# Attention pairs of the second block: a gate's Silu later in the order, the row maximum taken negated, and a PSUM bank for the second head's output

## The reference

```python
def forgetting_attention(q, k, v, f_logit, b_f):     # 16 heads of 64
    ...
        logits = jnp.einsum('bhqd,bhkd->bhqk', qi, k).astype(jnp.float32) * scale
        logits = logits + (Fi[..., :, None] - F[..., None, :])
        logits = jnp.where(q_pos[:, None] >= k_pos[None, :], logits, -jnp.inf)
        p = jax.nn.softmax(logits, axis=-1)
        return jnp.einsum('bhqk,bhkd->bqhd', p.astype(v.dtype), v)
...
        z = h @ w_in[l]
        u_a, v_a, g_a, q_b, k_b, v_b, g_b, f_b = jnp.split(z, pts, axis=-1)
        y_b = forgetting_attention(q_b, k_b, v_b, f_b, b_f[l]) * jax.nn.silu(g_b)
        y = jnp.concatenate([y_a, y_b], axis=-1) @ w_out[l]
```

## Time and profile before

| | us |
|---|---|
| median of 3 runs | 2638.51 |
| lowest, highest | 2636.88, 2639.52 |
| the profiled execution's own time | 2635.45 |
| its span | 2633.8 |
| pairs of the second block, about | 1991 to 2424 |

### The profile page before, as it was taken

One profiled execution on the slowest core, in us unless ns is written; L12 is line 12 of the kernel. 1 busy time (PEld: TensorE's weight loads), 2 busy tenths in 40 slices (PEclk: granted clock), 3 DMA queues, 4 the chain that ended last, 5 costly groups with the idle time before them and its releaser, 6 DMA issues.

```text
span 2633.8 us, 32288 instructions
## 1 busy us (share of the span) xinstructions
PE 2498.5 (95%) x11864; PEld 2014.6 (76%) x11864; DVE 1322.4 (50%) x1985; ACT 879.2 (33%) x1333; POOL 373.3 (14%) x363
## 2 busy tenths in 40 slices
PE   5899999999998999999999998799999999998997
PEld 2678888787887778888787886588877777776886
DVE  8655543377545655543367545725245444444433
ACT  4422222344322522222344222422224444444321
POOL 6300000012001500000012001203001112122000
PEclk8999999999998999999999998999999999999998
DMA  3355554211222355554211332133321222222332
GB/s 134 120 180 176 175 175 127 80 62 52 84 99 73 127 180 175 176 175 128 80 65 49 120 96 71 48 112 105 100 91 64 73 72 78 70 76 64 112 97 79
DMA packets 79437, 277.75 MB, mean 105 GB/s; under 512 B 8960, under 2 KB 9216, under 8 KB 78976
## 3 DMA queue, kind: packets, MB, share of 16 engines
q1 hardware_dynamic: 62496, 217.49, 25.5%
q0 software_dynamic: 14560, 55.06, 6.2%
q10 hardware_dynamic: 2304, 4.20, 0.4%
HBM read 270.41 MB, written 6.29 MB: 105 GB/s over the span
## 4 chain that ended last, share of the span: by engine, by line
PE 76%; issue 16%; DVE 5%; ACT 1%; POOL 1%; DMA 0%; ACTq 0%; DVEq 0%; SPq 0%; POOLq 0%
PE bank L275 23%; PE bank L277 23%; PE bank L276 23%; PE bank L1621 1%; DVE x_lo L909 1%; POOL sum L360 1%; PE bank L1586 1%; DVE w_lo L270 1%; PE bank L1582 1%; ACT w_hi L260 0%; DVE stats L1160 0%; PE bank L1584 0%; PE bank L1585 0%; PE bank L1587 0%; PE bank L1583 0%
## 5 line engine op out<-in xcount | busy, mean ns | idle before, releaser
L275 PE MATMUL bank<-x_lo,w_hi 128*128 128x512 f32 (+1 forms) x3088 | 1236.5, 400 | 48.1 <-DVE x_lo L909 21.3
L277 PE MATMUL bank<-x_hi,w_hi 128*128 128x512 f32 (+1 forms) x3088 | 1212.4, 393 | 0.0
L276 PE MATMUL bank<-x_hi,w_lo 128*128 128x512 f32 (+1 forms) x3088 | 1211.7, 392 | 0.0
L270 DVE TENSOR_TENSOR w_lo<-w_raw,w_hi 128x1024 fp32r<-128x1024 f32 (+2 forms) x398 | 493.5, 1245 | 841.7 <-ACT w_hi L260 839.4
L260 ACT ACTIVATE w_hi<-w_raw 128x1024 fp32r<-128x1024 f32 (+2 forms) x398 | 407.4, 1030 | 1004.9 <-PE bank L277 986.0
L275 PEld LDWEIGHTS bank<-x_lo,w_hi 128*128 128x128 f32 (+1 forms) x3088 | 579.6, 188 | 183.3 <-issue 44.2
L277 PEld LDWEIGHTS bank<-x_hi,w_hi 128*128 128x128 f32 (+1 forms) x3088 | 578.6, 187 | 132.1
L276 PEld LDWEIGHTS bank<-x_hi,w_lo 128*128 128x128 f32 (+1 forms) x3088 | 579.8, 188 | 121.6 <-issue 2.4
L347 POOL TENSOR_SCALAR probs<-probs,stats 128x128 f32<-128x128 f32 (+3 forms) x128 | 139.2, 1092 | 790.8 <-DVE stats L1154 790.6
L353 POOL DMA_DIRECT2D ada_w<-wada x96 | 51.2, 533 | 574.7 <-DVE ada_w L805 574.7
L612 ACT ACTIVATE probs<-bank,stats 128x128 f32<-128x128 f32 (+3 forms) x128 | 67.5, 527 | 183.7 <-DVE stats L1162 183.7
(11 more groups left out here) (267 smaller groups left out, 1972.5 us busy)
## 6 DMA issues: line engine op xcount, KB each, us to landing
w_raw<-stream SPq DMA_DIRECT2D x398, 512.0 KB, 3.5
ada_w<-wada POOLq DMA_DIRECT2D x96, 512.0 KB, 4.6
x_res<-xT SPq DMA_DIRECT2D x16, 256.0 KB, 5.2
outT<-x_res SPq DMA_DIRECT2D x16, 256.0 KB, 2.3
cond_b<-cond POOLq DMA_DIRECT2D x2, 1024.0 KB, 5.3
x_res_spill<-x_res ACTq DMA_DIRECT2D x8, 256.0 KB, 2.0
x_res<-x_res_spill ACTq DMA_DIRECT2D x8, 256.0 KB, 4.9
row_params<-rows POOLq DMA_DIRECT2D x1, 1536.0 KB, 8.3
```

Of the source, the lines that this page charges most:

```text
L270: nc.vector.tensor_tensor(out=WL[:, slot, :cols[n]], in0=RAW[:, slot, :cols[n]], in1=WH[:, slot, :cols[n]].bitcast(F32), op=ALU.subtract). ...
L275: nc.tensor.matmul(out, wh, xl, start=first, stop=False)
L276: nc.tensor.matmul(out, wl, xh, start=False, stop=False)
L277: return nc.tensor.matmul(out, wh, xh, start=False, stop=last)
```

## The change

1. ScalarE's `gate(p - 1)` moves from the head of the pass to behind `softmax_exp(…, 3)` and the first two `pt_hi` of the head that is finishing. After the loop it moves in the same way behind `pt_hi(last, 1)`.
2. VectorE's `pair_out(p - 1, 0)` moves from the head of the pass to behind `pt_lo(…, 1)`, and `recip(…, 2)` moves ahead of the row maximum of block 3. The same after the loop.
3. In the second block the row maximum is written negated by one instruction (`neg_max2`) in place of a maximum and a multiply.
4. The output of head (p, 1) goes to bank 3 in place of bank 2. Its first `pv` now waits for the head (p - 1, 1), and the first `pv` of head (p, 0) for head (p - 1, 0). The transposed v that shares bank 3 now waits for head (p - 1, 1) too. The first block passes its bank condition explicitly and with the same value as before.

```diff
@@ ScalarE, pair(p, first)
                 if not first:
-                    gate(p - 1)
                     softmax_exp(a - 1, 3, 1.0, BANKS_2)
                     pt_hi(a - 1, 0)
                     pt_hi(a - 1, 1)
+                    gate(p - 1)
                     pt_hi(a - 1, 2)
                     pt_hi(a - 1, 3)
@@ ScalarE, after the loop
-            gate(PAIRS - 1)
             softmax_exp(last, 3, 1.0, BANKS_2)
             for i in range(QB):
                 for k in MIX_BEHIND[i]:
                     mix2(k)
                 pt_hi(last, i)
+                if i == 1:
+                    gate(PAIRS - 1)
@@ VectorE
+            def neg_max2(hh, i):
+                dve.wait_ge(S["s_mm"], QB * hh + i + 1)
+                if i == 0:
+                    dve.wait_ge(S["p_norm"], QB * hh)
+                V.reduce_max(ST[:, 4 + i:5 + i], PS[BANKS_2[i]][:, :P * (i + 1)], axis=AXX, negate=True)\
+                    .then_inc(S["s_nb"], 1)
@@ VectorE, pair_out(p, b)
-                TT(out=g, in0=PS[2][0:DH2, :], in1=g, op=ALU.mult).then_inc(S["pv_out"], 1)
+                TT(out=g, in0=PS[2 + b][0:DH2, :], in1=g, op=ALU.mult).then_inc(S["pv_out"], 1)
@@ VectorE, pair(p, first); the other row_max of the pair become neg_max2 in place
                 if not first:
+                    recip(a - 1, 2)
+                    neg_max2(a - 1, 3)
+                    recip(a - 1, 3)
+                    pt_lo(a - 1, 0)
+                    pt_lo(a - 1, 1)
                     pair_out(p - 1, 0)
-                    row_max(a - 1, 3, 1.0, BANKS_2)
-                    recip(a - 1, 2)
-                    pt_lo(a - 1, 0)
-                    recip(a - 1, 3)
-                    pt_lo(a - 1, 1)
                     pt_lo(a - 1, 2)
                     pt_lo(a - 1, 3)
@@ VectorE, after the loop
+            recip(last, 2)
             for k in range(3):
                 mix2_lo(k)
-            pair_out(PAIRS - 1, 0)
-            row_max(last, 3, 1.0, BANKS_2)
-            recip(last, 2)
+            neg_max2(last, 3)
             recip(last, 3)
             for i in range(QB):
                 for k in MIX_BEHIND[i]:
                     mix2_lo(k)
                 pt_lo(last, i)
+                if i == 1:
+                    pair_out(PAIRS - 1, 0)
@@ TensorE
-            def pv(hh, i, out, vcols, v_ready):
+            def pv(hh, i, out, vcols, v_ready, bank_read):
...
                 if i == 0:
                     pe.wait_ge(S["v_lo"], v_ready)
-                    pe.wait_ge(S["pv_out"], hh)
+                    pe.wait_ge(S["pv_out"], bank_read)
@@
             def pv2(p, b, i):
-                pv(HB + 2 * p + b, i, PS[2][0:DH2, :], slice(DH2 * b, DH2 * (b + 1)), HB + p + 1)
+                pv(HB + 2 * p + b, i, PS[2 + b][0:DH2, :], slice(DH2 * b, DH2 * (b + 1)), HB + p + 1,
+                   HB + 2 * p - (b == 0))
@@
             def v_transpose2(p):
                 pe.wait_ge(S["v_out"], p + 1)
                 pe.wait_ge(S["v_lo"], HB + p)
+                pe.wait_ge(S["pv_out"], HB + 2 * p)
```

More of the change, by code:

```diff
@@ L1337, in pair @@
                 k_lo(p)
-                row_max(a, 0, 1.0, BANKS_2)
-                row_max(a, 1, 1.0, BANKS_2)
+                neg_max2(a, 0)
+                neg_max2(a, 1)
                 recip(a, 0)
                 half_split(s + 4, 0, i)
-                row_max(a, 2, 1.0, BANKS_2)
+                neg_max2(a, 2)
                 recip(a, 1)
-                row_max(a, 3, 1.0, BANKS_2)
+                neg_max2(a, 3)
                 recip(a, 2)
@@ L1357, in pair @@
                 half_split(s + 5, 0, i)
-                row_max(a + 1, 0, 1.0, BANKS_2)
-                row_max(a + 1, 1, 1.0, BANKS_2)
+                neg_max2(a + 1, 0)
+                neg_max2(a + 1, 1)
                 recip(a + 1, 0)
                 half_split(s + 5, 1, i)
-                row_max(a + 1, 2, 1.0, BANKS_2)
+                neg_max2(a + 1, 2)
                 recip(a + 1, 1)
@@ L1538, in pv1 @@
                             pe.wait_ge(S["kn_lo"], hh + 1)
-                        pv(hh - 1, i, PS[2], slice(0, VDIM), hh)
+                        pv(hh - 1, i, PS[2], slice(0, VDIM), hh, hh - 1)
                     pe.wait_ge(w_lo, before + 2)
@@ L1593, in layer @@
                         if h and i == 0:
-                            pv(HEADS * l + h - 1, 3, PS[2], slice(0, VDIM), HEADS * l + h)
+                            pv(HEADS * l + h - 1, 3, PS[2], slice(0, VDIM), HEADS * l + h, HEADS * l + h - 1)
                 last = HEADS * (l + 1) - 1
@@ L1600, in pr @@
                 def pr(i):
-                    return lambda: pv(last, i, PS[2], slice(0, VDIM), last + 1)
+                    return lambda: pv(last, i, PS[2], slice(0, VDIM), last + 1, last)
                 tile(l, T_OUT, 0, (S["mix_lo"], KT * l), MIX_ORDER,
```

## The result

The changed kernel takes 2612.71 us (median of 4 runs, 2608.43 to 2613.99), against 2639.02 us for the kernel before beside it (4 runs, 2636.88 to 2641.62). The ratio is 0.9897, 95% interval [0.988, 0.9914]: 26.3 us faster. The forecast was 2611.8 us, range 2608 to 2620. The profiled execution took 2613.98 us, its span is 2612.2 us.

A forecast was written before the change was run, and what follows sets the result against it. TensorE, busy 95% of the span, was taken to lose time only to waits and half-clock matmuls. Loop waits 14.2, half-clock falls 9.2 and after-loop gain 3.3 sum to 26.7 us, from 2638.51 to 2611.8 us, range 2608 to 2620.

The forecast's parts named there:

- The waits of the loop: TensorE's seven waits for pt_lo at the first pv of head (p, 1) vanish: 14.2 us, with 0.9 us to spare.
- Passes: Sign that the forecast is right: loop passes 54.4 us apart (56.45 - 2.02).
- The dips: Six falls to half clock behind the loop's waits go, 1.54 us each: 9.2 us, bounds 0 and 9.2.
- the dips stay: Rival, 8%: half clock follows from the short pieces behind step 7, not from the idle; 15.1 us won, 2623.4 us.
- The bank: Second bank takes away a 1.4 us wait for pair_out in the new order; in the old order worth nothing.
- The negation: Negated maximum drops a 0.15 us instruction from every block; nothing won in the loop; taken to cost 0.67 us.
- slow-negation rival: Rival, 3%: negated maximum far slower than the plain one; at five times its cost 13.6 us slower, 2652 us.
- After the loop: Waits and half clock after the loop: 2.1 + 2.4 - 1.2 = 3.3 us won, bounds -0.6 and 5.0.
- step 3 gone: After the loop, the Exp of block 3 starts 2.2 us earlier, taking 2.1 of the 2.19 us wait for split 3.
- a drain on each switch: Skill's rule of some 1.38 us more per table switch: step 8's wait 2.6 us, after-loop gain 1.4 us smaller.
- The sum: Loop waits, half-clock falls and after-loop gain: 14.2 + 9.2 + 3.3 = 26.7 us, median 2611.8 us.
- The range's bounds: Waits 14.2, half-clock falls 4.6 to 9.2, tail -0.6 to 5.0, runs' spread 1.6 us: 2608 to 2620 us.

The follow-up runs named there:

- b1: Kernel before, old order, with the gate's Silu replaced by a plain copy (no table loads there, result differs): 2618.84 us, ratio 0.9927.
- a4: Kernel before plus the new order of gate and pair_out and the second bank, with the two-instruction maximum: 2611.78 us, ratio 0.9897.
- a3: Kernel before with only the negation: all row maxima of the second block negated, old order, one bank: 2620.80 us, ratio 0.9937.
- c3: Kernel before with all second-block maxima negated and an unused instruction ahead of each on VectorE: 2626.55 us, ratio 0.9959.
- c2: Kernel before with only the maximum of block 3 of each head negated: 2633.96 us, ratio 0.9985.
- a2: Kernel before with only the second bank, in the old order: 2636.38 us, ratio 0.9994.
- a1: Kernel before with only the new order of gate and pair_out, one shared bank, two-instruction maximum: 2638.35 us, ratio 1.0001.
- c4: Changed kernel without its second bank (new order and negation, one shared bank): 2624.37 us, ratio 0.9947 to the kernel before.
- after_again: The changed kernel, unaltered, run once more as the standard of its chip: 2613.94 us, ratio 0.9907 to the kernel before.
- b2: Changed kernel with the last pair's gate and pair_out moved behind the last head's last pt_hi and pt_lo: 2612.18 us, ratio 0.9900 to the kernel before.
- b5: b2 with the splits 0 to 7 of tile T2_OUT moved ahead into the last pass: 2607.27 us, ratio 0.9882 to the kernel before.
- c1: b5 with the last pair_out and split 15 ahead of a weight split, last pv behind step 12: 2604.28 us, ratio 0.9875 to the kernel before.

## Why the prediction was right, point by point

- **The waits of the loop** (14.2 us): shown. All are gone, and both first `pt_lo` are done at 2029.92 + 0.70 = 2030.62, 0.6 us ahead of the `pv` (forecast: 0.9 us, for the first of them alone). The Exp of block 3 started 0.56 us after TensorE had come to that `pv` and now starts 2.30 us before it: 2.9 us earlier for 3.0 forecast. b1 shows the chain, a4 that order and bank are enough.
- **Passes**: 54.43 us forecast, 54.20 measured. The forecast took the wait alone off a pass, but a pass with a wait is some 0.2 us longer than its wait explains: with waits of 1.64 and 1.76 us (a3, c3) it takes 56.0 and 56.13 us, so without them 54.4, not 54.20.
- **The dips** (9.2 us): all six gone, and their price of 1.54 us shown anew by c2. The rival "the dips stay" is refuted by the changed kernel, where the same pieces stand behind step 7. For this change my reason held, since no wait is left. As a rule it was too coarse: I took a dip to come with any wait there, and a3 shows waits of 1.64 us without one. Why one wait has a dip behind it and another of the same length has none stays open.
- **The bank**: no gain alone (a2), needed by the new order (a1, c4). The wait without it was 2.1 us (1.7 with negation), where I had 1.4: a mis-sized term, by the handovers.
- **The negation**: nothing in the loop beside the other edits, as forecast (a4 equals the changed kernel). But the step was argued from "TensorE waits for none of the others", and for the edit alone, where TensorE does wait for this chain, it is wrong by 17 us. The slow-negation rival is excluded by the 0.69 us.
- **After the loop** (3.3 us): 2.8 us measured, which is 2449.14 - 2427.88 = 21.3 us from the end of the wait for split 0 to the end of that for split 15 before, and 2427.52 - 2409.04 = 18.5 after. The waits in between give 1.0 us of it (forecast 0.9: step 3 gone, and 1.18 us at step 8 for 1.2 forecast). The clock gives what is left, 1.8 us for 2.4 forecast, with 10.3 us of half clock turned into 3.4: a mis-sized term. Where the Trainium skill's ScalarE: Activation LUTs, section What ACT_TABLE_LOAD costs, puts a drain on each switch that would by the prediction's estimate have made that wait 2.6 us, the trace has the Silu 1.29 us after its load began (2030.18 and 2031.47 in pass 1; 2415.41 and 2416.70 after the loop). The measurement decides: no drain shows here.
- **The sum.** The two kernels can be laid side by side from the last start of TensorE that is marked "issue" ahead of the first pair's scores, up to the last wait (step 15). That start, in TensorE's timelines of the changed kernel and of the one before:

```profile
1994.71 0.47 PE L275 MATMUL bank<-x_lo,w_hi 128*128 128x512 f32 x1 [2.29 <-issue]
```

```profile
1988.56 0.70 PE L275 MATMUL bank<-x_lo,w_hi 128*128 128x512 f32 x1 [2.30 <-issue]
```

Before it is 2449.14 - 1988.56 = 460.6 us, after 2427.52 - 1994.71 = 432.8: 27.8 us for a forecast of 26.7. That is 14.2 + 9.2 + 2.8 and some 1.5 us, seven times the 0.2 us that a pass with a wait takes longer. The spans of the two profiled executions are only 21.6 us apart: the other 6.2 us lie ahead of the pairs, in code that the change doesn't touch. A part of it shows in one window, of the changed kernel and of the one before:

```profile
1304.00:1320.00 16.00, 14.54 (x54) 9.61 (x54) 6.46 (x18) 5.61 (x13) 4.29 (x4) 0.68 0.18 67
```

```profile
1304.00:1320.00 16.00, 14.54 (x85) 11.26 (x85) 10.12 (x24) 8.37 (x18) 4.30 (x4) 1.00 0.20 67
```

The clock's mean is 0.68 in the changed kernel and 1.00 in the one before, with the same 14.54 us busy and 1.46 idle. So it was at half clock for 0.32 / 0.5 x 16 = 10 us there, which made the code behind it 4.5 us late. The stretch of half clock starts less than 1 us behind that idle of 1.46 us, which both kernels have. after_again, a4, c4, b2, b5 and c1 have it too (0.68 or 0.79); a1, a2, a3, b1, c2 and c3 have 1.00. after_again had been expected to have it elsewhere if it were a matter of the single execution; it has it at the same place, so in these two executions it goes with the program. What makes it appear is open: the instructions there are the same, and no run changed that stretch alone.

The medians of the runs are 26.3 us apart for 26.7 forecast. That they meet so closely is in part luck: the loop gave 1.5 us more than forecast and the stretch behind it 0.5 less, and in the profiled executions untouched code took back 6.2 us, which no term of the sum has. Two bounds were also set too tightly. The range's bounds add up to 14.2 + 4.6 - 0.6 = 18.2 us at the least, which is 2620.3, and 2622 with the spread of 1.6, not 2620. And the clock was to be 1.00 from 1993 us on; a dip stood there at the head of the pairs before as well, and as all comes 6.2 us later now, its mean over 1994 to 2000 is 0.72.

## What to carry to other kernels

An instruction that nobody needs soon, at the head of an in-order engine's pass, is paid for by everything behind it; look for the first use of its result and put it not long before that. Moving it can make a buffer late that was free in time, so check each shared buffer against the new order: here the second bank was worth nothing alone, and the order nothing without it. Effects of edits don't add, least of all when a clock is among them: 0.4 us less of a wait won 17 us where the dips went with it (a3), and the same edit won nothing where no wait was left (a4 against the changed kernel).

## What the runs showed of the hardware that was not expected

- An idle of TensorE of about 2 us in a stream that is busy otherwise was followed by half clock (1.2 GHz) for 3.4 us, at 1.54 us each, in 20 of 21 passes; idles of 1.61 to 1.82 us at the same place were not, in 21 passes of three kernels; 1.81 to 1.84 us went both ways within one execution. Length alone isn't a rule: elsewhere an idle of 1.46 us had 10 us of half clock behind it in the changed kernel and none in the kernel before.
- c2's passes are 57.78 us with a dip and 56.23 us without, at the same wait.
- A stretch of 7 to 10 us at half clock came in untouched code in some kernels and not in others; the one of 10 us cost 4.5 us. So a difference of 5 us in one profile needs the region laid side by side before it is believed.
